# Dilated attention with final merge weights from compact statistics, worked in pairs of query tiles

## The reference, cut to what matters

```python
for g, (window, dilation) in enumerate(((128, 1), (512, 4), (2048, 16))):
    logits = q @ k.T * scale + bias            # banded, on the dilated subsequence
    lse = logsumexp(logits)
    o = exp(logits - lse) @ v
    outs.append(o); lses.append(lse)
wts = softmax(stack(lses), axis=0)             # over the three groups
o = sum(wts[..., None] * stack(outs), axis=0)
return (o * silu(z)) @ w_out
```

## Time and profile before

| | us |
|---|---|
| median of 3 runs (lowest, highest) | 3599.09 (3596.36, 3600.07) |
| the profiled execution's own time | 3601.79 |
| span of the profiled execution | 3599.9 |
| TensorE matmul busy | 3368.9 (94%) |
| TensorE weight load busy | 2641.3 (73%) |
| VectorE busy | 1907.0 (53%) |
| ScalarE busy | 1255.2 (35%) |
| GpSimd busy | 1149.0 (32%) |

### The profile page before, as it was taken

How to read it: one execution, slowest core, us unless ns; L and a number is a source line. 1 busy time by engine, 2 the same in 40 slices (tenths; PEclk the granted TensorE clock), 3 DMA queues, 4 the chain that set the end, 5 groups by cost and what they waited for, 6 DMA issues and landing times. The chain is left out here.

```text
span 3599.9 us, 50921 instructions
## 1 busy us (share of the span) xinstructions
PE 3368.9 (94%) x20086; PEld 2641.3 (73%) x20086; DVE 1907.0 (53%) x3730; ACT 1255.2 (35%) x2765; POOL 1149.0 (32%) x541
## 2 busy tenths in 40 slices
PE   5989999999999995989999899999999999999987
PEld 4767777777777773777877787777777777777775
DVE  3366555564646556639522524465455734465554
ACT  4334444443434443422221412244342322244421
POOL 1347666433323330423244122221115122221241
PEclk8999999999999996999999999999999999999998
DMA  5302121232332220321443310011002321011113
GB/s 133 68 27 64 49 61 49 61 114 87 97 103 62 80 86 13 115 91 53 158 176 100 111 45 24 24 35 29 24 24 88 111 62 30 28 37 35 30 44 121
DMA packets 309808, 247.54 MB, mean 69 GB/s; under 512 B 63877, under 2 KB 276889, under 8 KB 309578
## 3 DMA queue, kind: packets, MB, share of 16 engines
q10 hardware_dynamic: 107436, 130.26, 11.4%
q1 hardware_dynamic: 202142, 114.09, 11.2%
HBM read 207.92 MB, written 47.99 MB: 71 GB/s over the span
## 5 line engine op out<-in xcount | busy, mean ns | idle before, releaser
L2411 POOL TENSOR_TENSOR w_hi<-w_raw,one 128x1024 fp32r<-128x1024 f32 x170 | 361.2, 2124 | 2134.2 <-PE psum L1387 1017.6
L1387 PE MATMUL psum<-act_hi,w_hi 128*128 128x512 f32 (+1 forms) x1376 | 512.4, 372 | 23.9 <-DVE arena L1860 13.1
L2563 PE MATMUL psum<-act_hi,w_hi 128*128 128x512 f32 x1280 | 509.2, 398 | 13.4 <-ACTq L2826 5.8
L2563 PE MATMUL psum<-act_lo,w_hi 128*128 128x512 f32 x1280 | 515.6, 403 | 0.0
L1387 PE MATMUL psum<-act_lo,w_hi 128*128 128x512 f32 (+1 forms) x1376 | 512.1, 372 | 0.0
L1387 PE MATMUL psum<-act_hi,w_lo 128*128 128x512 f32 (+1 forms) x1376 | 509.8, 370 | 0.0
L2563 PE MATMUL psum<-act_hi,w_lo 128*128 128x512 f32 x1280 | 506.9, 396 | 0.0
L2414 POOL TENSOR_TENSOR w_lo<-w_raw,w_hi 128x1024 fp32r<-128x1024 f32 x170 | 435.9, 2564 | 13.3
L1387 PEld LDWEIGHTS psum<-act_hi,w_hi 128*128 128x128 f32 x1376 | 261.8, 190 | 74.9 <-DVE arena L1860 15.1
L1387 PEld LDWEIGHTS psum<-act_lo,w_hi 128*128 128x128 f32 x1376 | 261.9, 190 | 51.3 <-issue 13.7
L3277 DVE CUSTOM_DVE_ANT_0 arena<-psum,arena 128x128 f32<-128x128 f32 (+1 forms) x384 | 119.8, 351 | 338.0 <-issue 222.9
(11 more groups left out here) (369 smaller groups left out, 6120.9 us busy)
## 6 DMA issues: line engine op xcount, KB each, us to landing
w_raw<-in_attn_w_in SPq DMA_DIRECT2D x80, 512.0 KB, 3.7
w_raw<-in_w_in SPq DMA_DIRECT2D x64, 512.0 KB, 4.0
spare<-in_w_mod ACTq DMA_DIRECT2D x24, 1024.0 KB, 7.7
x<-arena ACTq DMA_DIRECT2D x24, 512.0 KB, 2.9
arena<-x ACTq DMA_DIRECT2D x24, 512.0 KB, 4.9
arena<-in_x ACTq DMA_DIRECT2D x16, 512.0 KB, 5.4
w_raw<-in_ssm_w_in SPq DMA_DIRECT2D x16, 512.0 KB, 3.7
arena<-mc_mat ACTq DMA_DIRECT2D x16, 512.0 KB, 3.6
```

The lines of the kernel that those rows point to most:

```text
L1387: ins = nc.tensor.matmul(psum[:, n % 2, 0:c], w[:, slot % 2, k * P:(k + 1) * P], a[:, k, c0:c0 + c], start=(m == 0), stop=(m == 23))
L2411: G.tensor_tensor(w_hi[:, par], w_raw[:, par], one[:, 0:1].to_broadcast([P, 1024]), ALU.mult).then_inc(slot_hi, 1)
L2563: ins = nc.tensor.matmul(psum[:, h % 2, :], w[:, (3 + j) % 2, k * P:(k + 1) * P], a[:, k, c:c + 512], start=(m == 0), stop=(m == 23))
```

## The change

Units go in pairs of one group: `turn_p`, `scores` and `outputs` each work on two units between two stretches of projection, so there are four such steps in a segment in place of eight, and LOG and PT hold one pair. WIDE and its two transposes for each unit are gone. `outputs` runs the two heads in turn (heads inside, key tiles outside). The row statistics stay compact in STAT (one column for each unit); once in a segment TensorE transposes them (32 rows x 128), VectorE copies them to STAT_ROWS, and ScalarE's queue writes them to DRAM in token order (one DMA for g = 2, four for the others) and loads them as 64 x 2 x 32. In the next pair's segment 0 VectorE and ScalarE compute the three final weights from them (3 + 1 + 5 small instructions); they go to DRAM, and four DMAs spread them over 64 partitions each into three full planes, 1.5 MB a head pair. Then there are three products, two sums and the gate, on full planes. The maximum is kept negated (subtract and minimum), so L3282 goes. Cut to its core:

```diff
-            def scores(hp, n, par):
+            def scores(hp, p, par):
+                if p % 4 > 0:
+                    pe.wait_ge(u_logits, 2 * NU * hp + 4 * p)
+                for a, (g, u) in enumerate(units_of(p)):
...
             def turn_p(hp, p):
+                pe.wait_ge(u_probs, 2 * NU * hp + 4 * p + 4)
...
             def outputs(hp, p):
+                pe.wait_ge(u_pt, NU * hp + 2 * p + 2)
+                if p >= 2:
+                    pe.wait_ge(u_evac, NU * hp + 2 * (p - 1))
...
+                    for i, t in enumerate(kt):
+                        for h in range(2):
+                            ins = nc.tensor.matmul(psum[64 * h:64 * h + 64, OB(p), a * P:(a + 1) * P],
...
-                pe.wait_ge(u_wide, NU * hp + n + 1)
-                for c in range(2):
-                    ins = nc.tensor.transpose(psum[:, OB(n), (c + 1) * P:(c + 2) * P],
-                                              WIDE[:, n % 2, c * P:(c + 1) * P], ident[:, :])
+                if p % 4 == 3:
+                    ins = nc.tensor.transpose(psum[0:4 * NT, OB(p), 2 * P:3 * P],
+                                              STAT[:, (3 * hp + si) % 2].rearrange("p a b -> p (a b)"), ident[:, :])
...
+            def spread_weights(hp, par):
+                act.wait_ge(w_moved, 80 * hp + 16)
                 for h in range(2):
+                    v = weight_rows[hp, 1, h]
+                    act.dma_start(QKV[64 * h:64 * h + 64, 1:3, :],
+                                  bass.AP(tensor=v.tensor, offset=v.offset, ap=[[0, 64], [2 * S, 2], [1, S]])).then_inc(w_moved, 16)
+                    v = weight_rows[hp, 0, h]
+                    act.dma_start(QKV[64 * h:64 * h + 64, buf(8, par), :],
+                                  bass.AP(tensor=v.tensor, offset=v.offset, ap=[[0, 64], [1, S]])).then_inc(w_moved, 16)
```

ScalarE's loop over i = 0 to 7 in a segment (p is `4 * si + i // 2`):

```diff
                 probs(hp, 4 * si)
+                if prev:
+                    put_stats(3 * hp + si - 1)
                 for i in range(8):
+                    if i % 2 == 0:
+                        while with_proj and 24 * (nh + 1) <= seg_at(hp, si, i + 1):
+                            evac(hp, h0 + nh, 1 - par, more)
+                            nh += 1
+                        take_pt(hp, p)
+                        if i < 6:
+                            probs(hp, p + 1)
+                    if i == 0 and prev:
+                        load_stats(3 * hp + si - 1)
+                    if i == 1 and si == 0 and prev:
+                        weight_exps(hp - 1)
+                        put_weights(hp - 1)
+                    if i == 2 and si == 0 and prev:
+                        spread_weights(hp - 1, 1 - par)
```

VectorE's merges in segment 0 (by i), and the gate's place in segment 1:

```diff
+            MERGES = {1: ("diff", "weights"), 4: (1,), 5: (2, 0), 6: ("two",), 7: ("three",)}
...
+                    if si == 1 and i == 4:
+                        gate(hp, 0)
+                    if i % 2 == 0 and i < 6:
+                        logits(hp, p + 1)
+                    if i % 2 == 0 and i > 0:
+                        evacuate(hp, p - 1, par)
...
+                if part == "diff":
+                    dve.wait_ge(st_moved, stats_loaded(3 * hp + 2))
...
+                if part == "weights":
+                    dve.wait_ge(c_act, hp + 1)
...
+                if part == 1:
+                    dve.wait_ge(w_moved, 80 * (hp + 1))
```

More of the change, by code:

```diff
@@ L1069, in build, with units_of, most_keys, OB @@
         NU = len(UNITS)
[L1071 to L1073 removed]
+        NQ = NU // 2
+        def units_of(p):
+            return [UNITS[2 * p], UNITS[2 * p + 1]]
+        def most_keys(p):
+            return max(len(key_tiles(g, u)) for g, u in units_of(p))
+        def OB(p):
+            return 6 + p % 2
         def key_tiles(g, u):
@@ L2688, in segment @@
                 turn_v(hp, si, par)
-                scores(hp, 8 * si, par)
-                for i in range(8):
-                    n = 8 * si + i
+                scores(hp, 4 * si, par)
+                for i in range(4):
+                    p = 4 * si + i
                     if with_proj:
[L2693 to L2697, removed]
+                        proj(hp, h0, at, seg_at(hp, si, 2 * i + 1))
+                        at = seg_at(hp, si, 2 * i + 1)
+                    turn_p(hp, p)
+                    if i < 3:
+                        scores(hp, p + 1, par)
                     if i > 0:
-                        outputs(hp, n - 1)
+                        outputs(hp, p - 1)
                 if with_proj:
@@ L2871, in take_pt, with probs @@
[L2871 to L2884, removed]
+            def probs(hp, p):
+                act.wait_ge(u_logits, 2 * NU * hp + 4 * p + 4)
+                st = STAT[:, (3 * hp + p // 4) % 2]
+                for a, (g, u) in enumerate(units_of(p)):
+                    for h in range(2):
+                        lg = LOG[:, a, h * 256:h * 256 + P * len(key_tiles(g, u))]
+                        nc.scalar.activation(lg, lg, ACT.Exp, scale=-1.0, bias=st[:, 2 + h, u:u + 1],
+                                             accum_out=st[:, h, u:u + 1]).then_inc(u_probs, 1)
@@ new lines, in put_stats @@
+            def put_stats(s):
+                act.wait_ge(st_rows, s + 1)
+                if s > 0:
+                    act.wait_ge(st_moved, stats_loaded(s - 1))
+                if s % 3 == 0:
+                    act.dma_start(stat_rows[s].rearrange("k (u c) -> (k u) c", u=NT), STAT_ROWS[0:4 * NT, :]).then_inc(st_moved, 16)
+                else:
+                    u_step, step, n = ((32, 256, 4), (8, 64, 16))[s % 3 - 1]
+                    for k in range(4):
+                        v = stat_rows[s, k]
+                        act.dma_start(bass.AP(tensor=v.tensor, offset=v.offset, ap=[[u_step, NT], [step, n], [1, P // n]]),
+                                      STAT_ROWS[NT * k:NT * k + NT, :].rearrange("p (n c) -> p n c", n=n)).then_inc(st_moved, 16)
@@ L2964, in segment_act @@
                 for i in range(8):
[L2965 to L2971, removed]
+                    p = 4 * si + i // 2
+                    if i % 2 == 0:
[12 more added lines that the diff above has]
+                        spread_weights(hp - 1, 1 - par)
                     if hp == 0 and si == 1 and i == 3:
@@ L3441, in _ @@
             pair_dve(HP - 1, 1, False)
-            evacuate(HP - 1, NU - 1, 1)
-            for part in ("diff", "n", "d0", "d2", "sum n", "sum d", 0, 1, "out"):
+            evacuate(HP - 1, NQ - 1, 1)
+            for part in ("diff", "weights", 1, 2, 0, "two", "three", "out"):
                 merge_all(HP - 1, 1, part)
```

343 lines of the change are left out of this document (152 added, 191 removed).

## The result

The changed kernel takes 3504.75 us (median of 4 runs, 3502.42 to 3508.67), the kernel before 3599.18 on the same chip: a ratio of 0.9742, 95% interval 0.9727 to 0.9756, or 94.4 us less.

What follows compares the result with a forecast made beforehand. TensorE's own stream and its waits were taken to bound the kernel. The terms summed to -76 us: 3601.8 - 76 = 3525.8, less 2.7 (profiled time above the median) is 3523 us; range 3487 to 3562.

Steps and rivals of the forecast that it cites:

- stream, with the statistics transposes: TensorE beside projection: 0.92 us saved a pair of units over 92 pairs, -84.6 us; statistics transposes add +2.5.
- old waits and their low clock: TensorE in the stream: some 25 us of waits plus 7 of low clock go, 3.4 stay: -28.6 us.
- projection waits, pairs 4 to 7: Segment 0, matmul 72 waits for ScalarE's late copy: 3.5 us plus 1.7 of clock, +21; pair 4's extra DMA issues +1.
- pairs 1 to 3, small operations beside splits: Small VectorE operations slowed beside GpSimd splits make half 2 late: stall of 2 us and half a us of clock, +7.5.
- pair 0: First head pair: keeps its long coefficient chain and meets the gate at one place, +3 us.
- spread late in the stream: Spread lands some 13 us after issue, so `outputs` of the fourth pair of units waits 0.5 us, seven times: +3.5.
- tail: From the last output to the merge's end: 31.8 us where it was 28, so +4 us.
- Rival (b): TensorE groups: once-paid parts are not paid once, only the WIDE transposes count, 35 us: 3573 us, chance 0.08.
- rival (c): Output matmuls: the two heads' column halves overlap when alternating, 30 us more gained: 3493 us, chance 0.06.
- (a): Projection at matmul 72: ScalarE is never late, no new waits, -112 us in all: 3487 us, chance 0.13.
- (d): Spread reads at a third of the plain rate and lands after 30 us, +125 us: 3648 us, chance 0.04.
- (e): TensorE's saved stream is replaced by waits at every pair of units (single buffers), no change: 3599 us, chance 0.03.

Runs made afterwards that it cites:

- experiment 4: Kernel before, with the merges' full-plane arithmetic and their two activations left out, the gate's multiplication kept: 3552.21 us, ratio 0.9865.
- experiment 1: Changed kernel, with the two projection halves of pairs 4 to 7 taken out ahead of the weights in segment 0: 3485.3 us, ratio 0.9677.
- experiment 7: Kernel of experiment 1 without the four transfers a head pair that spread the final weights: 3466.45 us, ratio 0.9618.
- experiment 3: Changed kernel, with four transposes of the identity added to each pair of units, 368 in all: 3541.64 us, ratio 0.9835.
- experiment 6: Changed kernel, with turns, scores and outputs parted again by unit in the two inner steps of each segment, no wait added: 3533.89 us, ratio 0.9809.
- experiments 5: Changed kernel, with an already met semaphore wait put back between the two units of each group of turns, scores and outputs: 3513.1 us, ratio 0.9757.
- experiment 2: Changed kernel, with output matmuls ordered heads outside and key tiles inside, so heads do not alternate: 3510.27 us, ratio 0.9749.

## Why the prediction was right

The forecast was 3523 us in a range from 3487 to 3562, and 3504.75 was measured: right side, right mechanism in the two largest terms, and the sum 18 us short of the gain. The smaller terms partly made up for each other, and not by foresight. By its steps, spans against the kernel before:

| step | predicted | found | from |
|---|---|---|---|
| stream, with the statistics transposes | -82.1 | -85.8 | marks: 3.66, 3.66, 3.86 us a segment, over 23 |
| old waits and their low clock | -28.6 | -26.7 | experiment 4 |
| projection waits, pairs 4 to 7 | +22 | +28.3 | marks; experiment 1 takes back 23.4 |
| pairs 1 to 3, small operations beside splits | +7.5 | 0 | marks; experiment 7 |
| pair 0 | +3 | -3.3 | marks |
| spread late in the stream | +3.5 | +3.8 | marks of pairs 1 to 3; at the convolution |
| last segment | -5.5 | -6 | marks |
| tail | +4 | +1 | marks |
| later stages | 0 | -4.0 | marks |

A segment's third value, 3.86, is the marks' 4.27 less the 0.41 that experiment 4 gains too. For pairs 0 to 3 "found" is the gain that is missing from the marks of an undisturbed head pair (11.2 us) and of experiment 4 together. The column sums to -92.7 where 93.6 were measured; the marks of pairs 0 to 3 are differences of small numbers, each good to about 1 us.

- **What bounds the kernel.** Right. Experiment 4 takes VectorE from 89 to 41 in 160 us and leaves the head pair at 160; the changed kernel's 154.9 us is the 155 that was written.
- **The stream.** Right, and the largest term. Of the 0.92 us a pair of units, 0.38 are the removed transposes (experiment 3 prices four at 0.41 in the trace and 33.6 us in all) and 0.54 the kinds paid once (experiment 6: 0.50 for three of the four, some 22 us over half of the steps). Rival (b) is out. What stayed undetermined in the prediction, wait or kind, is settled by experiments 5 and 6.
- **Heads alternating.** The choice to give it no gain was right. The Trainium skill (TensorE: Matmul & The Clock Gate, Part 3) tells of matmuls in different column groups that run at once; here two neighbours on different column halves save 0.05 us in twelve (experiment 2), not the 30 us of rival (c). The trace doesn't agree with the rule for full-depth matmuls of 128 columns with another weight load for each; what stands in the way isn't shown.
- **Old waits.** Right to 2 us.
- **The new wait.** Right in place, cause and number: matmul 72 of segment 0 in pairs 4 to 7. Its size was too low: 4.08 us where 3.5 was written, with 1.8 of clock behind it, and 7.0 in pair 4 (+1 had been given for its additional transfers, and it took 9.7 us in all, not 6.2; in experiment 1 it still loses 3.7, of which 3.1 go with the spread in experiment 7). The term that was left out is the VectorE operation that stands 2.27 us beside GpSimd's split; the prediction knew the effect from the earlier trace rows, and used it for pairs 1 to 3 alone. Other links of the chain were shorter than I had put them, so that the total came close. The Trainium skill (SBUF — State Buffer, "SBUF: two separate sides") has an exclusive lock between a GpSimd operation that reads SBUF and a VectorE one with two inputs in SBUF, where the second to start blocks until the first is through. The trace agrees: L3376 starts 0.16 us behind L2438 and ends 0.04 us behind it.
- **Pairs 1 to 3.** The term of +7.5 was wrong in its mechanism: TensorE has no wait there for a half that ScalarE had not taken out. Without the spread (experiment 7) segment 0 of these pairs gains 3.7 us over experiment 4, the undisturbed rate. What was lost, 3.8 us, came from the two convolution waits of 2.0 us, which are the spread's, where no wait over 1 us was forecast.
- **Pair 0.** The +3 did not come either; the pair gained 3.3 us beyond the undisturbed rate. By the list of waits experiment 4 still has 8.8 us of waits in it (3.44 before transposes of probabilities and 1.54 at a projection matmul among them), the changed kernel 4.8. Which part of the change removes them is not tested.
- **The spread.** Its time alone was right: 9.8 us from the first issue to the merge in the tail, 10.2 written. In the stream it is 9.8 to 10.0 in the changed kernel, where the stall has let the modulation loads go ahead, and 14.5 in pairs 5 to 7 of experiment 1, where it runs behind them (13 written). The 5.6 us that the prediction worked out from the Trainium skill (DMA: Bandwidth & Descriptors, Anatomy of one DMA), whose fit is for one transfer issued from GpSimd, is too short for the four transfers. That it would delay the copy that `outputs` waits for was half right: the copy came late, but in pairs 1 and 2, and what waited for it was the convolution. So the +3.5 met the 3.8 by luck.
- **The other rivals.** (a) is out by the four waits, (d) by the 9.8 us of the spread, (e) by the head pair that is 5.8 us shorter.
- **Tail.** 1 us longer instead of 4: statistics put and load took 4.6 us, from 1321.36 to the first VectorE operation on them at 1325.94, where 6.7 were written.
- **Later stages.** The prediction had nothing for them. Some 4 us came in stages whose instructions are unchanged, within the 7.8 us by which these stages differ among the traces; no run here says why they do.

## What to carry to other kernels

Where one engine's stream bounds a kernel, look at what it pays at each change from one kind of instruction to another: here small matmuls of one kind put side by side saved 0.5 us a step, and semaphore waits that were met cost nothing. Relief of an engine beside the bound is worth just the waits it caused (here, and at the end of the stage, where it bounds); take them from the list of waits, with the low clock behind each. When a new chain is put into an engine that works in order, move what others wait for ahead of it: three lines that took two finished halves out first were worth another 23 us. A transfer can also cost at a place that does not read it: VectorE waited 0.8 us for the spread, and TensorE then 2.0 us for a copy that stood behind the merge in VectorE's order.

## What was not expected of the hardware

- A VectorE operation of 64 x 32 elements takes 0.18 us, and 2.27 beside a GpSimd split of 2.39 that started 0.16 earlier. That happened in the same place with the chain earlier (2.28, experiment 1).
- The three changes of kind of TensorE cost 0.50 us together, at full clock, with no wait between them.
- While the modulation weights land (891 to 896 us; the spread is issued from 896.9 on), the DMA share is 1.03 and 331 GB/s move; TensorE's projection runs there, behind its wait, at a granted clock of 0.66. In experiment 1, where the spread is under way together with them and TensorE does not wait, it runs at full clock (2.4 GHz) beside a DMA share of 1.12 (362 GB/s), so the low clock goes with the wait and not with such traffic:

```profile
888.00:893.00 5.00, 5.00 (x24) 4.14 (x23) 0.00 (x0) 2.35 (x8) 2.30 (x2) 1.00 1.12 362
```
